# Output projection of the last 26 tiles in pairs with seven block products, and m kept as fp32

## The reference, cut to what matters

```
m = jnp.concatenate([o_gla, o_rwkv], -1).astype(x.dtype)   # 1024 channels
m = jnp.einsum('btc,cd->btd', m, w_out)                    # w_out is 1024 x 1024
x = x + rms_norm(m, norm_post)
```

## Time and profile before

| what | us |
|---|---|
| time, median of 3 runs | 2375.19 (2369.25 to 2376.35) |
| profiled execution, span | 2370.8 |
| PE busy in it | 2287.6 (96%) |
| ACT, DVE, POOL busy | 1427.8, 1308.5, 569.9 |
| first matmul of tile 7, the first of the last 26 | at 2093.51 |
| end of the last matmul | at 2362.88 |

### The profile page before, as it was taken

How to read it: one execution, slowest core, us unless ns; L and a number is a source line. 1 busy time by engine, 2 the same in 40 slices (tenths; PEclk the granted TensorE clock), 3 DMA queues, 4 the chain that set the end, 5 groups by cost and what they waited for, 6 DMA issues and landing times. The chain is left out here.

```text
span 2370.8 us, 72009 instructions
## 1 busy us (share of the span) xinstructions
PE 2287.6 (96%) x31129; PEld 1721.6 (73%) x31129; DVE 1308.5 (55%) x2477; ACT 1427.8 (60%) x2820; POOL 569.9 (24%) x1070
## 2 busy tenths in 40 slices
PE   6999999999999998889999999999999998999998
PEld 5777777777777766778888887888888874544443
DVE  6444444444444443566777776767777775432222
ACT  8466666666666645546776666666676774543323
POOL 0000000000000001155555554455555555000000
PEclk9999999999999998999999999999999999999999
DMA  7112222222211111123222222222222234354453
GB/s 244 67 55 73 73 73 69 69 81 91 73 54 54 54 63 48 43 52 78 76 71 73 69 67 76 76 76 76 76 67 74 56 93 145 115 167 150 152 160 125
DMA packets 198779, 204.74 MB, mean 86 GB/s; under 512 B 108608, under 2 KB 151936, under 8 KB 194112
## 3 DMA queue, kind: packets, MB, share of 16 engines
q1 hardware_dynamic: 196304, 184.41, 26.3%
q10 hardware_dynamic: 2160, 15.73, 1.8%
HBM read 119.81 MB, written 80.28 MB: 84 GB/s over the span
## 5 line engine op out<-in xcount | busy, mean ns | idle before, releaser
L675 PE MATMUL d<-h,w_hi 128*128 128x256 f16 (+1 forms) x3264 | 527.4, 270 | 9.8 <-DVE w_lo L1133 8.1
L675 PE MATMUL d<-h,w_lo 128*128 128x256 f16 (+1 forms) x1632 | 436.7, 270 | 0.0
L1816 POOL TENSOR_TENSOR r_inv_tmp<-r_inv 64x30 f32<-64x30 f32 (+14 forms) x480 | 259.5, 541 | 435.0 <-DMA r_inv<-scratch_blocks 398.7
L675 PEld LDWEIGHTS d<-h,w_hi 128*128 128x128 f16 x3264 | 315.1, 98 | 55.6 <-issue 14.9
L1855 PE MATMUL r_d<-h,w_hi 128*128 128x256 f16 (+1 forms) x1824 | 297.0, 269 | 0.8 <-DVE carry_s L2394 0.8
L1818 POOL TENSOR_TENSOR r_inv<-r_inv,r_inv_tmp 64x30 f32<-64x30 f32 (+14 forms) x480 | 278.2, 580 | 37.6
L1855 PE MATMUL first<-h,w_hi 128*128 128x256 f16 x1664 | 282.5, 273 | 0.0
L1855 PE MATMUL r_d<-h,w_lo 128*128 128x256 f16 (+1 forms) x912 | 241.6, 269 | 0.0
L1855 PE MATMUL first<-h,w_lo 128*128 128x256 f16 x832 | 227.2, 273 | 0.1
L1759 POOL MEMSET r_run_s<- 128x128 f16 x1 | 0.2, 204 | 930.6 <-POOLq L360 930.6
L1855 PEld LDWEIGHTS r_d<-h,w_hi 128*128 128x128 f16 x1824 | 171.9, 98 | 37.2 <-issue 14.7
(11 more groups left out here) (323 smaller groups left out, 4792.3 us busy)
## 6 DMA issues: line engine op xcount, KB each, us to landing
h<-in_x SPq DMA_DIRECT2D x33, 512.0 KB, 3.8
r_ops<-in_x SPq DMA_DIRECT2D x33, 512.0 KB, 4.2
out_y<-r_ops SPq DMA_DIRECT2D x33, 512.0 KB, 2.9
scratch_hT<-h SPq DMA_DIRECT2D x16, 1024.0 KB, 7.0
h<-scratch_hT ACTq DMA_DIRECT2D x15, 1024.0 KB, 7.0
scratch_mg<-m_hl SPq DMA_DIRECT2D x33, 256.0 KB, 2.0
r_zr<-scratch_zr SPq DMA_DIRECT2D x33, 256.0 KB, 3.6
r_bon<-scratch_bonus SPq DMA_DIRECT2D x33, 256.0 KB, 4.7
```

Of the source, the lines that this page charges most:

```text
L675: mm = pe.matmul(out, lhs(k, a, w), rhs(k, a, w), start=(n == 0), stop=(n == len(terms) - 1))
L1816: step(pool.tensor_tensor(tmp, inv[0:n, 0:u, u:u + 1].to_broadcast([n, u, w]), inv[0:n, u:u + 1, u + 1:32].to_broadcast([n, u, w]), ALU.mult))
```

## The change

1. m is stored as fp32 (`scratch_m`, the same 256 KB per half tile). The four splitting jobs of the two phases are gone. A tile's halves are split where they are used.
2. Tiles 0 to 6 ("singles") are projected as before, in the 84 first rooms. SP's `get_m` loads a half each into two buffers, ACT's `m_high` and DVE's `m_low` (two operations each) make the fp16 pairs. The 24 last rooms of body 17 stay empty.
3. Tiles 7 to 32 go in 13 pairs. With the tokens of a pair as 2 block rows, and channels and output columns in 2 halves, seven block products of 12 matmuls (Strassen's scheme) stand for the 2 x 48 matmuls of two tiles. PE takes 84 matmuls for a pair in place of 96. They use two banks, and three products add onto one that is already in a bank, after it has been copied out.
4. The sums of weight blocks are made once, in body 16: SP `get_tw`, POOL `tw_sum`, ACT `tw_high`, DVE `tw_low`, four rounds of four 256 KB loads and four operations on each engine.
5. Each pair needs sums of m blocks (POOL `part_sum` x4), splits (ACT `part_high` x7, DVE `part_low` x7), copies and sums of products (ACT `kept` x2, DVE `made` x5), squares (ACT x4), `scaled` (POOL x4), the factor without the table load (ACT `o_ln`, `o_exp`) and `done` (DVE x4). These lists are written out in `tail_jobs`; a pair's parts are made during the pair before it ("ahead").

The core of the diff, cut:

```
+SINGLES = 7
+NPAIR = (NT - SINGLES) // 2
+TW_AT = (("get_tw", 8, 0), ("tw_sum", 9, 4), ("tw_high", 9, 4), ("tw_low", 9, 4))
+PRE_AT = (("get_pair", 12, 0), ("part_sum", 14, 4), ("part_high", 14, 7), ("part_low", 14, 7))
+def tail_jobs(p):
+    more = p + 1 < NPAIR
+    def ahead(job, *ns):
+        return [(job, (p + 1, n)) for n in ns if more]
+    return {
+        "PE": [("product", (p, n)) for n in range(7)],
+        "ACT": [("kept", (p, 0)), *ahead("part_high", 0, 1), ("square", (p, 0)), ("kept", (p, 1)),
+                *ahead("part_high", 2, 3, 4), ("square", (p, 1)), *ahead("part_high", 5, 6), ("square", (p, 2)),
+                ("o_ln", (p, 0)), ("o_exp", (p, 0)), ("square", (p, 3)), ("o_ln", (p, 1)), ("o_exp", (p, 1))],
+        "DVE": [("made", (p, 0)), *ahead("part_low", 0, 1), ("made", (p, 1)), *ahead("part_low", 2, 3),
+                ("made", (p, 2)), *ahead("part_low", 4, 5), ("made", (p, 3)), ("summed", (p, 0)),
+                *ahead("part_low", 6), ("done", (p, 0, 0)), ("done", (p, 0, 1)), ("made", (p, 4)), ("summed", (p, 1)),
+                ("done", (p, 1, 1)), ("done", (p, 1, 0))],
+        "POOL": [*ahead("part_sum", 0, 1), ("scaled", (p, 0)), *ahead("part_sum", 2, 3), ("scaled", (p, 1)),
+                 ("scaled", (p, 2)), ("scaled", (p, 3))],
+    }
...
+            def get_tw(k):
+                if k:
+                    sp.wait_ge(t_dve.sem, AT["tw_low", (k - 1, 3)])
...
+                for j in range(4):
+                    row = (4 * (j // 2) + k) * P
+                    sp.dma_start(o_stage[:, j, :], t["w_out"][row:row + P, (j % 2) * 512:(j % 2 + 1) * 512])...
+            def get_pair(p):
...
+                else:
+                    sp.wait_ge(t_dve.sem, AT["part_low", (p - 2, 6)])
...
+                for n in range(4):
+                    half, i = divmod(n, 2)
+                    sp.dma_start(m_own[s][n], m_d[tile + i][:, half])...
...
+            for p in range(NPAIR):
+                for i in range(2):
+                    get_x(SINGLES + 2 * p + i)
+                    if i == 0 and p + 1 < NPAIR:
+                        get_pair(p + 1)
+                for i in range(2):
+                    put_y(SINGLES + 2 * p + i)
...
+            def pair_product(arg):
...
+                if n < 2:
...
+                elif n in (2, 4):
+                    pe.wait_ge(t_act.sem, AT["kept", (p, n // 2 - 1)])
+                else:
+                    pe.wait_ge(t_dve.sem, AT["made", (p, {3: 0, 5: 1, 6: 2}[n])])
...
+            def tw_high(arg):
...
+                act.wait_ge(t_pool.sem, AT["tw_sum", (k, 3)])
...
+            def part_high(arg):
+                p, n = arg
+                s, x = p % 2, PART_ORDER[n]
+                if n == 0:
+                    act.wait_ge(h_in[s].sem, h_in[s].at(8 - s + 4 * (p // 2) + 3, 1))
...
+                if n >= 3:
+                    act.wait_ge(t_pool.sem, AT["part_sum", (p, n - 3)])
```

More of the change, by code:

```diff
@@ L214, in mean @@
         if i < len(back):
-            steps.extend((j, back[i]) for j in ("squares", "rnorm", "gate", "high_m", "low_m", "put_mg"))
+            steps.extend((j, back[i]) for j in ("squares", "rnorm", "gate", "put_mg"))
     def turn(i, h):
@@ L273, in own_mean @@
         def own_mean(i):
-            steps.extend((j, own[i]) for j in ("squares", "rnorm", "gate", "high_m", "low_m", "put_mg"))
+            steps.extend((j, own[i]) for j in ("squares", "rnorm", "gate", "put_mg"))
         steps += [("get_h", 0), ("get_h", 1)]
@@ L297, in a_steps @@
         steps.append(("put_zr", b))
-        steps.extend((j, own[1]) for j in ("high_m", "low_m", "put_mg"))
+        steps.append(("put_mg", own[1]))
         return steps
@@ L1205 @@
 """.split()
-POOL_BODY = "-invert".split()
+POOL_BODY = "-invert out out out out out out out out".split()
 SP_BODY = """
@@ L1275, in opening_jobs @@
                     yield from script_jobs(name, arg, b, int(n or 1))
-OUT_UNITS = [(tile, n) for tile in range(NT) for n in range(12)]
+SINGLES = 7
+NPAIR = (NT - SINGLES) // 2
+OUT_UNITS = [(tile, n) for tile in range(SINGLES) for n in range(12)]
+TW_AT = (("get_tw", 8, 0), ("tw_sum", 9, 4), ("tw_high", 9, 4), ("tw_low", 9, 4))
[16 more added lines that the diff above has]
+    }
+TAIL = {e: [j for p in range(NPAIR) for j in tail_jobs(p)[e]] for e in ("PE", "ACT", "DVE", "POOL")}
+AT = {}
+for _e, _tw, _pre, _n in (("PE", "", "", 0), ("ACT", "tw_high", "part_high", 7), ("DVE", "tw_low", "part_low", 7),
+                          ("POOL", "tw_sum", "part_sum", 4)):
+    _first = [(_tw, (k, n)) for k in range(4) for n in range(4) if _tw] + [(_pre, (0, n)) for n in range(_n)]
+    AT.update({job: n + 1 for n, job in enumerate(_first + TAIL[_e])})
 def out_jobs():
@@ L1286, in put @@
         jobs.append((pos, len(jobs), job, arg))
-    for tile in range(NT):
+    for tile in range(SINGLES):
         p = 12.0 * tile
+        if tile:
+            put(p - 8.0, "get_m", tile)
+        put(max(p - 5.0, 0.0), "m_high", tile)
+        put(max(p - 5.0, 0.0), "m_low", tile)
         put(max(p - 8.0, 0.0), "fetch", tile)
@@ L1319, in pe_program @@
             if job == "room":
-                jobs.append(("out", next(units)))
+                jobs += [("out", u) for u in itertools.islice(units, 1)]
             elif job == "piece":
@@ L1350, in side_program @@
                     jobs += [(j, k) for k in range(2 * KT) if OW_AT[k] + at == arg]
+            if "get_m" in mine and arg == M_FROM:
+                jobs.append(("get_m", 0))
+            for j, at, each in TW_AT:
+                if j in mine and 0 <= arg - at < 4:
+                    jobs += [(j, (arg - at, n)) for n in range(each)] or [(j, arg - at)]
+            for j, at, each in PRE_AT:
+                if j in mine and at == arg:
+                    jobs += [(j, (0, n)) for n in range(each)] or [(j, 0)]
             if "fetch" not in mine:
@@ new lines, in summed, with done @@
+            def summed(arg):
+                p, i = arg
+                s = st[:, (SINGLES + i) % 2]
+                dve.wait_ge(t_act.sem, AT["square", (p, i + 2)])
+                dve.tensor_tensor(s[:, 2:3], s[:, 0:1], s[:, 1:2], ALU.add).then_inc(*t_dve.up(0))
+            def done(arg):
+                p, i, h = arg
+                tile = SINGLES + 2 * p + i
+                slot, n = tile % 2, tile // 2
+                src, m = ((c_11, 0), (c_12, 2), (c_21, 3), (c_22, 1))[2 * i + h]
+                dve.wait_ge(t_act.sem, AT["o_exp", (p, i)])
+                dve.wait_ge(xc_in[slot].sem, xc_in[slot].at(n, 1))
+                dve.wait_ge(t_pool.sem, AT["scaled", (p, m)])
+                x = x_c[:, slot, h * 512:(h + 1) * 512]
+                dve.scalar_tensor_tensor(out=x, in0=src, scalar=st[:, slot, 3:4], in1=x, op0=ALU.mult,
+                                         op1=ALU.add).then_inc(*t_dve.up(0))
```

343 lines of the change are left out of this document (256 added, 87 removed).

## The result

The changed kernel took 2485.17 us (median of 4 runs, 2481.43 to 2493.12) beside 2374.42 us for the kernel before (4 runs): ratio 1.0481, 95% interval 1.0462 to 1.0500 (the two medians by themselves give 1.0466). It is 4.8% slower; the forecast was 2477 us.

What follows compares the result with a forecast made beforehand. PE was taken to bound the long phases and the end. On the profiled span, 2370.8 - 2 (freed splits) + 35 (body 16) + 69 (tail) = 2472.8; the median 4.4 above gave 2477 us, range 2405 to 2505.

Steps and rivals of the forecast that it cites:

- Freed splits: Both long phases: removing the splits of m saves 2 us, between 0 and 5, capped by PE's idle time.
- Body 16: Weight rounds holding ACT and DVE, and seven splits ahead of `even`, delay the recurrence's end: +35 us, bounds +18 and +42.
- The loads' landing: Tail: the next pair's block loads, queued behind `put_y`, land 9.0 us after its second issue at about T+5.1.
- H: Tail: the time the next pair's block loads land, forecast T+14.1, lowest T+11, highest T+15.
- T: Tail: the start of a pair's product 0, from which the forecast counts its times.
- The gap ahead of product 4: Tail, each pair: product 4, due at T+10.4, starts at H+2.7 = T+16.8, so PE stands 6.4 us.
- The clock behind it: Tail: after PE's 6.4 us stand, half speed for 3.4 to 5.3 us costs 1.7 to 2.6 us; 2.1 taken.
- The gap ahead of product 0: Tail: no such gap forecast; DVE's splits priced at 0.69 us, a possible POOL and DVE lock of 1.1 us a pair left out.
- The end: After the last pair's products: sums, factor, two `done` and the store take about 8.9 us, where it was 7.9.
- The reason for the period: Tail: late loads behind the stores, the wait for product 4 and the clock loss make 26.7 us a pair, against 20.72.
- step 4: Tail: the next pair starts at H+10.5 = T+24.6; this pair's `done` ends 5 us behind that, so the loop repeats.
- The faster rival: Tail and body 16: helpers keep ahead of PE, product 4 never waits, weight rounds hide; 2344 us, chance 0.08.

Runs made afterwards that it cites:

- thin sums: The changed kernel with POOL's weight-block sums in body 16 over 2 columns in place of 512: 2476.48 us, ratio 1.0442.
- POOL light: The changed kernel with POOL's `part_sum` and `scaled` over 2 columns in place of 512: 2463.94 us, ratio 1.0375.
- the last version: The 2368.86 us version plus `made` 0 of the next pair ahead of the last two `done`, and pair 0's splits in two groups: 2367.92 us, ratio 0.9993.
- The best version: The changed kernel with spread weight rounds, early block loads, finer waits, `kept` 0 ahead of the last square, pair 1's loads at point 17: 2368.86 us, ratio 0.9989.

## Why the prediction was right, and where its terms were off

- **Direction, place and size** hold. Both blocks are there: stalls a pair ahead of product 4, and body 16. The profiled execution came to 2482.8 for a sum of 2472.8; the median stood 2.4 us above the span and not 4.4, which took 2 us of the miss away.
- **Freed splits** (-2, bounds 0 to -5): by chunk 62 the recurrence was 10.5 us ahead, of which 6.5 by chunk 57 (at 1955 us), about what the idle time of the second stretch allows and above my bound of 5. The other 4 came in the last chunks, to which that stretch says nothing: there PE had more idle time, the 3.65 us of the earlier trace rows among it. Leaving the splits out of the kernel before gave 7 of the 10.5 in a profiled execution, or all of it counted within the second phase, but only some 4 us in the medians; why the medians show less stays open.
- **Body 16** (+35): from chunk 62 to pair 0 the delay grew from -10.5 to +35.4, so it cost 45.9. With the recurrence ahead, the rounds ended at 2033.4, 2052.9, 2066.1 and 2089.9, that is 8.9, 7.7, 8.1 and 4.8 us before my times: the jobs ahead of them came 10.5 us sooner, so 5.7 were lost in them, 2 of these in round 4, whose low splits ran beside the next POOL sums (2.37 us for two and 1.75 for one, where the first round's took 1.29 and 0.69). From round 4's end to pair 0 it was 39.0 us for my 33.8: PE waited 7.10 us for `even` behind the seven splits, which I had at 4; the other 2 us are not traced. Spreading the rounds gave 25 back, with pair 0's splits moved as well, so it was mostly their spacing; thin sums gave 10, so POOL's time is less than half of it. That the place came out right is luck: the two errors cancelled, -10.5 and +45.9 make +35.4, my two terms +33.
- **The loads' landing**: H was T+13.7 (2210.41 to 2224.1) for T+14.1. From the second store's issue to the last landing it was 8.6 us for my 9.0. The estimate of 6.8 us for the burst from the fit in the Trainium skill, "DMA: Bandwidth & Descriptors" (Anatomy of one DMA), an H of 11.9, does not agree with it; the page gives that fit for a single DMA issued by GpSimd, and these are six in SP's queue.
- **The gap ahead of product 4**: 5.2 us on average (4.9 to 5.6) for 6.4, as H came sooner and product 4 started at H+2.3 (I had 2.7). The clock behind it took 1.9 us on average for 2.1. The working cites the earlier trace rows for full clock behind the 3.48 us; those rows don't have that stretch, but the trace shows 1.00 from 958 to 962 us.
- **The gap ahead of product 0** was not in the sum: `part_low` 6 stands behind `summed` 0 on DVE and beside `scaled` on POOL, and takes 1.77 us for the 0.69 I gave it. That is what POOL's operations do to DVE's, which the prediction left out of its sum; with POOL light the period was 1.6 us shorter. It counts through the stores and not through the gap. One lap in the pair shown, from one pair's last matmul to the next pair's, was 7.0 us to the second store (I had 5.1, as the split stands ahead of the last `done`), 8.6 to the landing (9.0), 2.3 to product 4 (2.7) and 9.6 for products 4 to 6 (9.9). The period was 27.3 on average for 26.7, and the first pair took 27.3 for 25.7. 12 periods and the last pair: 345.4 for 337.5.
- **The end**: 8.5 for 8.9.
- **The reason for the period**: I had the loop right, as one that feeds back through the stores (step 4). The experiments bear this out most sharply where a gap went and the time stayed.
- **The faster rival** needed `get_pair` not to stand behind `put_y`. With that done, and the rounds spread, the time was still 0.4% above the kernel before: of the pair's 2.59 us of matmuls less, the gap left 0.84 (a period of 19.88 for 20.72), and pair 0 started 8.5 us later and took 30.3 us. Its other half, that helpers with busy sums of 9 to 12 us keep inside 18 us, failed as well: a period of 19.45 for 18.13, by DVE's stretched operations as far as the last version's stretch shows it.

The best version's profiled execution shows the balance: pair 0 at 2102.4 (+8.9 to the tile 7 of before), the tail 267.3 us for 277.3 (-10.0), span 2369.7 for 2370.8. Its ratio, 0.9989, has an interval that ends just below 1. All the scheduling bought the way back to where the kernel had been.

## What to carry to other kernels

A loop over buffers is a cycle, and its period is found by following one lap of it (store, load, split, product, sum, store), not by adding up the gaps: a gap outside the lap can be removed for nothing gained, and one inside only moves if its data stays late. Put loads for two steps ahead in front of the stores in an in-order queue, and give a staged load as many points as its landing takes. When work goes from an engine that is full to engines that seem half idle, price their operations as they are beside each other: here a split that takes 0.69 us alone takes about twice that beside POOL's sums, and of the 12.5% of matmuls saved in a pair, half was gone in the best version (19.45 us where the matmuls alone take 18.13 and had taken 20.72); the weight sums in body 16 cost about as much as the rest gave.

## What the runs showed of the hardware

- POOL's sum of two 128x512 fp32 blocks took 1.27 us alone and 1.59 to 1.73 beside DVE's operations with two inputs in SBUF; DVE's went from 0.69 to as much as 1.78. DVE's sums with one input in PSUM (`made`) stayed at 0.68 throughout.
- After PE had stood 4.9 to 5.6 us, its granted clock was at 0.50 for some 4 us, which cost 1.6 to 2.2 us of work. Behind gaps of 1.6 us, in the middle of the tail of the version with early loads, it was 1.00.
- Four loads of 256 KB issued behind two stores of 512 KB and one x load landed 5.7 us after the last of them was issued.
